# Expert steps of a hybrid decoder layer: the neighbouring step's turns placed between parts of the gate/up products

## The reference

```python
a = jnp.einsum("nd,edf->nef", h, w_gate)
bu = jnp.einsum("nd,edf->nef", h, w_up)
hid = jax.nn.silu(a) * bu * combine[..., None].astype(h.dtype)
return jnp.einsum("nef,efd->nd", hid, w_down)
```

## Time and profile before

| | |
|---|---|
| median of 3 runs | 954.86 us (954.0 to 956.1) |
| profiled execution | 956.44 us, span of its instructions 954.53 us |
| granted TensorE clock, mean | 0.982 of full speed |
| busy: PE, PEld, DVE, ACT, POOL | 95%, 86%, 48%, 37%, 24% of the span |
| expert steps in the profile | first gate/up product at 709.35 us, last instruction at the end of the span |
| memory traffic | 118.6 MB, 124 GB/s on average; 246 to 335 GB/s in most of the slices of the expert steps |

### The profile page before, as it was taken

The page is one execution under the profiler, slowest core; times in us unless marked ns, Lnnn a source line. Parts: engine busy times, 40 slices in busy tenths (PEclk is TensorE's granted clock), DMA queues, the critical chain, the costliest instruction groups (busy, mean ns, idle before and its releaser), DMA issues. The chain is left out here.

```text
span 954.5 us, 16245 instructions
## 1 busy us (share of the span) xinstructions
PE 910.3 (95%) x5417; PEld 821.1 (86%) x5418; DVE 460.9 (48%) x842; ACT 357.8 (37%) x622; POOL 229.5 (24%) x241
## 2 busy tenths in 40 slices
PE   7899998999998999999999999999899999999993
PEld 7777776787998999999999999999887888888882
DVE  5677876443222222222232245443887768587550
ACT  5566555210232112111121141221436667577551
POOL 2434221345120000000000020000043357355552
PEclk9899999999999999999999999999999999999997
DMA  7321310200301201102111026963538898989733
GB/s 244 107 71 46 119 51 23 69 1 1 102 1 67 68 33 51 48 33 66 33 37 62 22 68 194 321 228 109 149 123 286 288 329 268 327 246 335 246 53 45
DMA packets 57359, 118.57 MB, mean 124 GB/s; under 512 B 7469, under 2 KB 32749, under 8 KB 57296
## 3 DMA queue, kind: packets, MB, share of 16 engines
q1 hardware_dynamic: 49824, 100.10, 30.6%
q0 software_dynamic: 7488, 17.85, 8.3%
HBM read 105.37 MB, written 23.00 MB: 134 GB/s over the span
## 5 line engine op out<-in xcount | busy, mean ns | idle before, releaser
L1402 ACT ACTIVATE gate<-psum 128x352 f32<-128x352 f32 x48 | 22.2, 465 | 211.6 <-PE psum L75 211.6
L73 PE MATMUL psum<-w_hi,hT_hi 128*128 128x512 f32 (+3 forms) x224 | 84.6, 378 | 4.0 <-ACT w_hi L559 2.1
L75 PE MATMUL psum<-w_hi,hT_lo 128*128 128x512 f32 (+3 forms) x224 | 80.8, 361 | 0.0
L74 PE MATMUL psum<-w_lo,hT_hi 128*128 128x512 f32 (+3 forms) x224 | 80.6, 360 | 0.0
L2174 DVE TENSOR_TENSOR hT_lo<-room,hT_hi (+1 forms) x32 | 72.1, 2290 | 16.1 <-ACT hT_hi L1871 16.1
L73 PE MATMUL psum<-hT_hi,x_xT_hi 128*128 (+1 forms) x192 | 77.5, 404 | 1.5 <-DVE x_xT_lo L2328 1.1
L73 PE MATMUL psum<-hT_hi,w_hi 128*128 128x352 f32 x240 | 77.4, 323 | 0.0
L74 PE MATMUL psum<-hT_lo,w_hi 128*128 128x352 f32 x240 | 76.9, 321 | 0.0
L75 PE MATMUL psum<-hT_hi,w_lo 128*128 128x352 f32 x240 | 76.9, 321 | 0.0
L74 PE MATMUL psum<-hT_lo,x_xT_hi 128*128 (+1 forms) x192 | 75.2, 391 | 0.0
L75 PE MATMUL psum<-hT_hi,x_xT_lo 128*128 (+1 forms) x192 | 75.1, 391 | 0.0
(11 more groups left out here) (348 smaller groups left out, 2332.5 us busy)
## 6 DMA issues: line engine op xcount, KB each, us to landing
room<-in_w_gu SPq DMA_DIRECT2D x16, 2048.0 KB, 11.6
dn_raw<-in_w_dn SPq DMA_DIRECT2D x16, 1024.0 KB
g_w_raw<-in_w_ab SPq DMA_DIRECT2D x15, 768.0 KB, 4.3
xT_chunk<-in_xT SPq DMA_DIRECT2D x8, 528.0 KB, 3.7
x_in<-in_x SPq DMA_DIRECT2D x8, 512.0 KB, 3.5
out_y<-y SPq DMA_DIRECT2D x8, 512.0 KB, 3.2
hn_rows<-squares SPq DMA_DIRECT2D x8, 512.0 KB, 3.2
o_w_raw<-in_w_out_t SPq DMA_DIRECT2D x7, 512.0 KB, 6.7
```

The lines of the kernel that those rows point to most:

```text
L73: eng.matmul(out, lh, rh, start=first and k == 0, stop=False)
L74: eng.matmul(out, lh, rl, start=False, stop=False)
L75: mm = eng.matmul(out, ll, rh, start=False, stop=last and k == nk - 1)
L1402: act.activation(gate[:, (ab + c) % 2, :], bank(psum, gate_pair(ab, c))[:, 0:TC], ACT.Sigmoid).then_inc(gated.sem, 1)
```

## The change

The arithmetic stays. The order of the parts of a step is another on three engines.

- TensorE, step s: first half of the gate/up products of s (4 of 8 blocks, 12 matmuls), hidden turn of s-1, token turn of s+1, one more block of s (3 matmuls), down products of s-1, the last three blocks of s (9 matmuls). In step 0 the token turn of step 1 stands between the two halves. The hidden turn and down products of the last step come behind the loop.
- ScalarE, step s: hidden of s-1, tokens of s+1, the gate/up halves that became free with step s-1, evict of s-1, silu of s, and new down weights in two halves. The condition is that of step s-1's plan, and the down weights are now those of the expert after next.
- VectorE, step s: hidden of s-1, tokens of s+1, the second down half, the gate/up halves, hid of s, the first down half. Expert 0's down weights, expert 1's second gate/up half and expert 1's down weights are made within steps 0 and 1.
- SyncE: `load_down` waits for both halves.

```diff
--- before.py
+++ after.py
@@ -1718,8 +1718,8 @@
                 sp.dma_start(gu_flat[:, i % 2], io["w_gu"][i], max_dma_last_dim=4 * D).then_inc(gu_in[i % 2], DMA)
 
             def load_down(i):
-                dn_hi_made.wait(sp, i - 2)
-                dn_lo_made.wait(sp, i - 2)
+                dn_hi_made.wait(sp, 2 * i - 3)
+                dn_lo_made.wait(sp, 2 * i - 3)
                 sp.dma_start(dn_raw[:, i % 2], io["w_dn"][i], max_dma_last_dim=4 * D).then_inc(dn_in[i % 2], DMA)
 
             for d in range(KD):
@@ -1900,10 +1900,9 @@
             act.wait_ge(made, 3 * KD)
             up_high(1, 0)
 
-            def down_high(n):
-                buf = n % 2 if isinstance(n, int) else bass.ds(n % 2, 1)
-                act.wait_ge(dn_landed, n + 1)
-                act.activation(dn_hi[:, buf], dn_raw[:, buf], ACT.Copy).then_inc(dn_hi_made.sem, 1)
+            def down_high(n, k):
+                buf, part = (n % 2 if isinstance(n, int) else bass.ds(n % 2, 1)), slice(k * D, (k + 1) * D)
+                act.activation(dn_hi[:, buf, part], dn_raw[:, buf, part], ACT.Copy).then_inc(dn_hi_made.sem, 1)
 
             def tokens_high(s, j):
                 up_made.wait(act, s - 2)
@@ -1924,33 +1923,43 @@
 
             def step(s, r):
                 j = r % 2
-                plan = splits_of(act, s)
+                if not first(s):
+                    plan = splits_of(act, s - 1)
+                    hidden_high(s - 1)
+                tokens_high(s + 1, 1 - j)
+                if not first(s):
+                    with act.If(plan % 2 > 0):
+                        n = plan // 4 + 2
+                        act.wait_ge(gu_landed, n + 1)
+                        for half in range(2):
+                            up_high(n, half)
+                    evict(s - 1, out[:, 1 - j, :])
                 up_made.wait(act, s)
                 hid_made.wait(act, s - 1)
                 act.activation(silu, bank(psum, 2 + j)[:, 0:DE], ACT.Silu, scale=slot_wr[:, 1, bass.ds(s, 1)]).then_inc(silu_made.sem, 1)
-                tokens_high(s + 1, 1 - j)
-                with act.If(plan % 2 > 0):
-                    n = plan // 4 + 2
-                    act.wait_ge(gu_landed, n + 1)
-                    for half in range(2):
-                        up_high(n, half)
-                hidden_high(s)
                 if not first(s):
-                    evict(s - 1, out[:, 1 - j, :])
-                    with act.If(plan // 2 % 2 > 0):
-                        down_high(plan // 4 + 1)
+                    with act.If(plan % 2 > 0):
+                        n = plan // 4 + 2
+                        act.wait_ge(dn_landed, n + 1)
+                        for k in range(KF):
+                            down_high(n, k)
 
             def last(used):
+                hidden_high(used - 1)
                 evict(used - 1, last_out)
 
             act.wait_ge(g_shifted, 1)
             act.activation(g_exp[:, :, :], g_exp[:, :, :], ACT.Exp).then_inc(g_exped, 1)
             up_high(1, 1)
             act.wait_ge(evicted, 3 * KD)
-            down_high(0)
+            act.wait_ge(dn_landed, 1)
+            for k in range(KF):
+                down_high(0, k)
             act.wait_ge(e_shifted, 1)
             act.activation(ratio[:, :], ratio[:, :], ACT.Exp).then_inc(e_exped, 1)
-            down_high(1)
+            act.wait_ge(dn_landed, 2)
+            for k in range(KF):
+                down_high(1, k)
             tokens_high(0, 0)
             act.wait_ge(found_made, 2)
             act.activation(slot_wr[:, :, :], bank(psum, 7)[:, 0:2 * EVEN].rearrange("p (a s) -> p a s", a=2)[:, :, 0:PLANNED],
@@ -2037,18 +2046,19 @@
                         mm = pe.transpose(bank(psum, half)[:, k * P:(k + 1) * P], xg[:, r, ks], ident[:, :])
                     mm.then_inc(xT_made.sem, 1)
 
-            def up(s, j, n):
+            def up(s, j, n, k0, k1):
                 buf = bass.ds(n % 2, 1)
-                hid_made.wait(pe, s - 2)
-                for half in range(2):
-                    xT_hi_made.wait(pe, 2 * s + half)
-                    xT_lo_made.wait(pe, 2 * s + half)
-                    gu_hi_made.wait(pe, n * 2 + half)
-                    gu_lo_made.wait(pe, n * 2 + half)
-                    h = half * KH
-                    mm = product(pe, bank(psum, 2 + j), lambda k: (xT_hi[:, j, h + k, :], xT_lo[:, j, h + k, :]),
-                                 lambda k: (gu_hi[:, buf, h + k], gu_lo[:, buf, h + k]), KH, first=half == 0, last=half == 1)
-                mm.then_inc(up_made.sem, 1)
+                half = k0 // KH
+                if k0 == 0:
+                    hid_made.wait(pe, s - 2)
+                xT_hi_made.wait(pe, 2 * s + half)
+                xT_lo_made.wait(pe, 2 * s + half)
+                gu_hi_made.wait(pe, n * 2 + half)
+                gu_lo_made.wait(pe, n * 2 + half)
+                mm = product(pe, bank(psum, 2 + j), lambda k: (xT_hi[:, j, k0 + k, :], xT_lo[:, j, k0 + k, :]),
+                             lambda k: (gu_hi[:, buf, k0 + k], gu_lo[:, buf, k0 + k]), k1 - k0, first=k0 == 0, last=k1 == KD)
+                if k1 == KD:
+                    mm.then_inc(up_made.sem, 1)
 
             def hidden_turn(s):
                 hid_made.wait(pe, s)
@@ -2061,8 +2071,8 @@
                 buf = bass.ds(n % 2, 1)
                 hidT_hi_made.wait(pe, s)
                 hidT_lo_made.wait(pe, s)
-                dn_hi_made.wait(pe, n)
-                dn_lo_made.wait(pe, n)
+                dn_hi_made.wait(pe, n * 2 + 1)
+                dn_lo_made.wait(pe, n * 2 + 1)
                 out_made.wait(pe, s - 1)
                 for half in range(2):
                     part = [slice(k * D + half * HD2, k * D + (half + 1) * HD2) for k in range(KF)]
@@ -2073,11 +2083,16 @@
             def step(s, r):
                 if not first(s):
                     pair = experts_of(pe, s)
-                    up(s, r % 2, pair // NE)
-                token_turn(s + 1, (r + 1) % RING)
-                if not first(s):
+                    up(s, r % 2, pair // NE, 0, KH)
+                    hidden_turn(s - 1)
+                    token_turn(s + 1, (r + 1) % RING)
+                    up(s, r % 2, pair // NE, KH, KH + 1)
                     down(s - 1, pair % NE)
-                hidden_turn(s)
+                    up(s, r % 2, pair // NE, KH + 1, KD)
+
+            def last_step(used):
+                hidden_turn(used - 1)
+                down(used - 1, experts_of(pe, used) % NE)
 
             def stay_warm(n, b=4):
 
@@ -2122,9 +2137,11 @@
             spread_factors(0)
             token_turn(0, 0)
             spread_factors(1).then_inc(found_made, 1)
-            up(0, 0, 0)
+            up(0, 0, 0, 0, KH)
+            token_turn(1, 1)
+            up(0, 0, 0, KH, KD)
             pe.wait_ge(plan_made, 1)
-            over_steps(pe, step, lambda used: down(used - 1, experts_of(pe, used) % NE))
+            over_steps(pe, step, last_step)
 
         @block.vector
         def _(dve):
@@ -2232,10 +2249,11 @@
             def over_last(a, n):
                 return a.unsqueeze(2).broadcast_to([P, a.shape[1], n])
 
-            def down_low(n):
-                buf = n % 2 if isinstance(n, int) else bass.ds(n % 2, 1)
-                dn_hi_made.wait(dve, n)
-                dve.tensor_tensor(dn_lo[:, buf], dn_raw[:, buf], dn_hi[:, buf].bitcast(F32), ALU.subtract).then_inc(dn_lo_made.sem, 1)
+            def down_low(n, k):
+                buf, part = (n % 2 if isinstance(n, int) else bass.ds(n % 2, 1)), slice(k * D, (k + 1) * D)
+                dn_hi_made.wait(dve, n * 2 + k)
+                dve.tensor_tensor(dn_lo[:, buf, part], dn_raw[:, buf, part], dn_hi[:, buf, part].bitcast(F32),
+                                  ALU.subtract).then_inc(dn_lo_made.sem, 1)
 
             dve.wait_ge(squared, KD)
             dve.wait_ge(summed, KD)
@@ -2359,29 +2377,36 @@
 
             def step(s, r):
                 j = r % 2
-                plan = splits_of(dve, s)
+                if not first(s):
+                    plan = splits_of(dve, s - 1)
+                    hidden_low(s - 1)
+                tokens_low(s + 1, 1 - j)
+                if not first(s):
+                    if isinstance(s, int) and s == 1:
+                        up_low(1, 1)
+                    with dve.If(plan // 2 % 2 > 0):
+                        down_low(plan // 4 + 1, 1)
+                    with dve.If(plan % 2 > 0):
+                        for half in range(2):
+                            up_low(plan // 4 + 2, half)
+                if first(s):
+                    for k in range(KF):
+                        down_low(0, k)
+                if isinstance(s, int) and s == 1:
+                    for k in range(KF):
+                        down_low(1, k)
                 silu_made.wait(dve, s)
                 hidT_made.wait(dve, s - 1)
```

(18 more changed lines are left out.)

## The result

The changed kernel takes 959.24 us (median of 5 runs, 958.62 to 961.48) against 955.28 for the kernel before on the same chip: a ratio of 1.0045, 95% interval 1.0027 to 1.0062. It is slower by 4.0 us in the medians and about 4.3 by the ratio, where 951.0 and a range up to 955.2 had been forecast.

The account below looks back on a forecast made before the run. TensorE was taken to bound the expert steps; gains of 1.9 (start), 1.5 (middle) and 1.5 (end), less 1.0 for late releases and held evicts, gave 3.9 us: profiled 956.44 to 952.5, median 951.0, range 949.2 to 955.2.

Parts of the forecast that it names:

- the queue behind the load of expert 3: SyncE at the start: expert 3's load goes out at 723.8 instead of 719.9, wanted at 739, so 15 us remain.
- the cover of the hidden rows: TensorE's down products: hidden rows' low part ready at 4.01 us into the step, products due at 4.53, cover 0.5.
- the down products of the end: Last down products on TensorE, behind the loop: expected from 12.5 to 15.6 us after step 23's start.
- Start: TensorE between steps 0 and 1: step 1's products start at 715.8, a gain of 1.9 us.
- Period: TensorE's undisturbed step stays 9.40 us, bounded by one slow interval either way, 0.09 us per step or 2 us in all.
- Uneven places: Four late places in the middle, made by VectorE's longest chain, were to go: 1.5 us gained.
- Late releases and held evicts: Steps behind one-step experts and ScalarE's evict: 1.0 us taken off the gain.
- Down halves: Splitting down copies: ScalarE 2.04 against 1.87 a pair, VectorE 0.15 more a pair, all beside TensorE.
- End: Step 23's start to the last scatter-add issue: 17.6 us instead of 19.07, a gain of 1.5 us.
- the first: Rival, chance 0.12: GpSimd's scatter-adds become the bound and the kernel is slower, 953.5 to 958.
- The second: Rival, chance 0.16: weight halves late by 0.5 us at seven places, 3.5 us lost, 953 to 955.
- The third: Rival, 0.70 together with the forecast: gains only at the two ends, 1.9 + 1.5, middle as uneven as before, 951.5.

Follow-up runs that it names:

- down-load run: Changed kernel with SyncE's load of expert 2's down weights ahead of the gate/up load of expert 3: 955.1 us, ratio 1.0007 to the kernel before.
- combined kernel: Changed kernel with expert 2's down load first, down products behind six gate/up blocks, and 6 and 8 small matmuls at the end: 951.03 us, ratio 0.9948.
- short fillers: Changed kernel with 6 small matmuls into an unread bank before the last hidden turn and 8 before the last down products: 958.67 us, ratio 1.0027.
- the start undone: Changed kernel with step 1's token turn behind all of step 0's gate/up products instead of between the halves: 961.4 us, ratio 1.0058.
- the fillers: Changed kernel with small matmuls before the last hidden turn and last down products: 10 and 14, 960.62 us, ratio 1.0069; 6 and 8, 958.67 us, 1.0027.
- the down halves together: Changed kernel with both halves of VectorE's down split behind the hidden product, the second not moved to the next step: 971.02 us, ratio 1.016.

## Why the prediction was wrong, step by step

Three steps failed: the queue behind the load of expert 3, which was not followed to its end (4.4 us); the cover of the hidden rows, from which the release was left out (about 2.6 us over the periods); and the down products of the end, priced at full clock (1.5 us).

- **Start: right, and its gain void.** 715.8 forecast, 715.52 measured. "SyncE's load of expert 3 waits for this split and goes out at 723.8" was right too: 723.40. What failed is the next clause, "behind it in the queue are the down loads of experts 2 and 3. Expert 3 is wanted at 739, so 15 us remain". I gave the due time of the first load in the queue alone. Expert 2's down weights stood behind it. They went out at 723.89, 3.6 us later than before (720.34), and were now asked for at 735.3, 3.9 us earlier than before (739.15); they were seen to have landed only at 738.66. That step, a queue named but not followed to its end, cost 4.4 us in step 3, of which 1.55 is the lower clock behind it. The down-load run gave 4.3 of it back in its trace, 3.6 in the medians.
- **Period: a term missed.** "So the period stays 9.40", with one slow interval in place of two. There are two: the first down product has one of its own, because its operands are released only as it is due. What failed is "Cover 0.5" for the hidden rows. The two times were right (low part 4.06 us into the step against 4.01, down products at 4.60 against 4.53), but the release between them takes 0.54, and it was left out, although the same text takes 0.46 for a release ahead of 812.59. So there was no cover at all: the down products start when they are released, mostly 0.02 late, and the weight load can't be taken ahead. The bound of one slow interval a step, "or 2 us in all", was in the text, and I took its better end. It measured 0.10 a step, 2.2 us in all, and with the 0.02 the period is 0.12 longer.
- **Uneven places: right.** The four late places of before are gone in the changed kernel; one of about 0.35 us is left, at the down products at 896.84, where VectorE made the low part of the hidden row late. In the combined kernel 22 periods take 207.6 against 208.3 before.
- **Late releases and held evicts: over-sized.** I had taken 1.0 us off. No row shows a wait of TensorE for the gate/up halves, and no wait of `evict` other than for TensorE.
- **Down halves: right.** VectorE's cost 1.22 us each, 2.44 a pair against 2.29, just the 0.15 that I had taken. ScalarE's cost 2.00 a pair; the one piece took 1.90 to 1.94 and not the 1.87 that I had taken from the gate/up pair. Without the half moved to the next step the kernel loses 11 us.
- **End: mis-sized by 2.3 us.** 17.6 was forecast, 19.85 measured. The hidden turn came at 11.05 where 11.0 was forecast; the low part ended 1.70 behind it instead of 1.26, because VectorE started 0.35 behind ScalarE's end, and with a release of 0.54 the down products started at 13.3 instead of 12.5. Then the failed term: 3.07 us for the down products, taken from a stretch at full clock. They took 4.6 at the lower clock, behind standstills of 1.4 and 1.8 us with only two transposes between. "Now 2.7 us of it is bare, and this is included" counted the idle time and not what it does to what follows. The run with the short fillers puts it at 1.56 us. The trace of the down-load run, whose clock stayed up there, gives the same, so this loss does not come in every execution.

The sum: start -1.9, period +2.6 (22 times 0.12), uneven places -1.5, the one late down block +0.35, step 3 +4.4, end +0.8, and -0.2 before step 0 and behind the last issue: together +4.6. The traces differ by 5.3. The other 0.7 lies in the steps that take 9.60 instead of 9.52, in which gate/up products follow each other after 0.2335 instead of 0.230 us. I found no cause for the two spacings; this part stays open.

The rivals: the first, the scatter-adds as the bound, did not happen. Its chance of 0.12 was nearly all that the forecast had left for a slower kernel. GpSimd's waits for them fell from 74.0 to 59.9 us and nobody waited for GpSimd, so the slower time had nothing to do with the mechanism to which I had given it. The second, late weight halves, did not happen either. The third said that the two ends give 3.4 us in any case; the start's part was handed back in step 3, and the end lost instead of gaining. The middle, which it took to stay as uneven as before, lost 6.6.

## What to carry to other kernels

When an issue on a queue is delayed, work out the due time of everything behind it in that queue, and compare the order of the queue with the order of need: three issues in another order were worth about 4 us here. Count a cover from the end of the producing instruction plus the release, 0.54 us here: what is left after that is the cover. Leave some more where the weights of the next product are to be loaded ahead; one more block, 0.7 us, was enough here. And where a change bares a wait of TensorE, look in the trace at what the clock did behind waits of that length, and price what follows at that clock too.

## What the runs showed of the hardware

**The clock behind short waits.** TensorE's waits in the expert steps, with the granted clock in the 3 us that followed: 1.51 us before the last down products of the kernel before (at 937.14), 1.00; 1.59 with the start undone, 1.00; 1.97 in step 3 with the down products behind six blocks, 0.51; 2.67 and 2.81 in step 3 of the changed kernel in two executions, about 0.5 for most of the time; 2.48 and 2.50 in step 3 with the fillers, and 3.71 with the down halves together, 0.5 as well. A pair of 1.36 or 1.37 and 1.81 with two transposes between was followed by 0.50 in five traces, and by 1.00 in that of the down load first. In the changed kernel each fall slowed the products for some 3 us and cost about 1.55; at the end of the kernel with the start undone all twelve down products were slow, at a cost of 2.2. I had expected nothing of that from waits so short. The same pair of waits at both levels shows that their length alone does not decide. The memory traffic was as high in the window at 1.00 as in that at 0.51. The two windows, of the kernel with the start undone and of the one with six blocks:

```profile
742.00:745.00 3.00, 2.61 (x11) 2.20 (x12) 2.95 (x4) 3.00 (x3) 0.00 (x0) 1.00 1.02 414
```

```profile
742.00:745.00 3.00, 3.00 (x8) 2.33 (x8) 2.95 (x2) 2.51 (x2) 0.00 (x0) 0.51 1.00 373
```

**A release** from the end of VectorE's low part to the first down product took 0.53 to 0.57 us in every step of the changed kernel.

**A weight load that can't be taken ahead** costs 0.10 us for a block of products, 0.33 instead of 0.23 for the first interval, without any wait in the table of waits. With the low part 1.22 us ahead it was taken ahead, with 0.53 to 0.57 it was not. It appears only in the row of PEld, as a load that starts together with its product.

**Small float32 matmuls** of 128 x 128, not of the type fp32r of the products, appeared as two records of about 0.12 us each.
